# Four more pairs of up units in seven block products, and three input sums moved to GpSimd

## The chip, the cores and the metric

The kernel runs on one core of one Trainium2 chip. The metric is the time of one execution on the device, in microseconds (us). Before the change it is 2313.94 us, the median of three runs (2313.18 to 2315.19).

## What is computed

Two small language-model blocks, one after the other, on an input of 512 tokens by 1024 features, in float32. The first block has two layers (a hybrid of sliding-window attention and a gated delta rule; a gated linear recurrence), each followed by a layer norm, an MLP and another layer norm. The second has two more layers with their own mixers and feed-forward parts. The change touches only the MLP of the first block, which runs twice (`l` = 0 and 1):

```python
def sqrelu_mlp(x, w1, w2):
    h = jax.nn.relu(x @ w1)          # 512x1024 by 1024x4096
    return (h * h) @ w2              # 512x4096 by 4096x1024

for layer in range(2):
    x = layer_norm(a * x + mixer(x), ln1_g[layer], ln1_b[layer])
    x = layer_norm(a * x + sqrelu_mlp(x, mlp_w1[layer], mlp_w2[layer]), ...)
```

## The kernel before

**Layout.** Features lie on the partitions and tokens in the free dimension. `X` holds 8 tiles of 128 features by 512 tokens. A *unit* is 128 output features: its weights are 8 blocks (K blocks) of 128x128, one slot of 1024 columns. `XHS` and `XLS` are the input split into a high part (`XH`, rounded to fp32r) and the rest (`XL`). Weights are split in the same way into `WH` and `WL`. A product is then three matmuls: high by high, high by rest, rest by high (`three`, lines 331 to 333; `product_pe`, lines 1150 to 1152). An ordinary unit takes 8 x 3 matmuls of 512 columns.

**The weight ring.** `plan_units` lists all units in the order in which TensorE uses them. Unit `u` lies in slot `u % 7`. SyncE loads it (`load_weights`, line 274) once unit `u - 7` is done, ScalarE makes the high part (`split_hi`, line 289) and VectorE the rest (`split_lo`, line 304). `WL` and `RAW`, the loaded weights, share their memory. The splits are issued by hand between the other steps of the two engines, four or five units ahead of TensorE (`split_for`).

**The MLP.** It has four parts (q = 0 to 3), each with 8 up units (`w1`) and 8 down units (`w2`). An up unit's result is evicted by ScalarE (relu, line 1231), squared by VectorE (line 1292), and split into `H`, high on ScalarE (line 1222), rest on VectorE (line 1276). The down units of q take it as input and are added to `X`. Up to now parts 0 and 1 run unit by unit, then come the 8 down units of part 0. Parts 2 and 3 run in *pairs*: two up units by 512 tokens by 1024 inputs are a 2x2 by 2x2 product of blocks, done with seven block products instead of eight (Winograd's form of Strassen). A block product is 4 K blocks x 3 matmuls of 256 columns. Between the products of a pair stand two down units of the part before.

**What a pair needs.** Sums of weights, made by GpSimd (`weight_sums`, four operations of 128x512, lines 259 to 265) once the pair's first and fourth slot are loaded: `S1` to `S4`, which take two slots of the ring (`s12`, `s4`) that aren't loaded. And sums of inputs, made once in a layer: T1 (X late front less X early front), T2 (X late back less T1), T4 (X early back less T2), T3 (X late back less X late front), each 128x1024 (four tiles of 256 tokens), and each split into high part and rest. T3's parts overwrite `XH` and `XL`, so T3 waits for the last ordinary up unit. T1, T2, T4 are made by VectorE at line 1127 in the second part, after units 1 to 3 of it; ScalarE makes their high parts after units 3 to 5, VectorE their rests after 4 to 6. T3 is made at the beginning of the down units of part 0.

**Copies out of PSUM.** In a pair TensorE runs M1, M5, a third product, then U2 on top of M1's bank. It may overwrite or add to it only when ScalarE has copied M1 (`p_copy`, line 1247). M5's copy is line 1251, U2's is line 1256.

**Order.** Every engine's instructions run in the order in which they are written here; they meet through semaphores. The queue order on ScalarE ahead of the first pair is this:

```python
            split_hi(act, PAIR_AT[l, 0] + 5)
            s1, s2, s3, c1, c2 = pair_tiles()
            for p, (q, j) in enumerate(PAIRS):
                ...
                act.wait_ge(p_mm, (l, p, "M1"))
                ...
                act.e.activation(s1, PS[BANK_P][:, EARLY], ACT.Copy).then_inc(*p_copy.at((l, p, "M1")))
```

**Ahead of the MLP.** The layer norm before it is worked in two halves of 256 tokens. Its last steps are ScalarE's write of `X` (line 626, signal `x_norm`) and VectorE's rest of the input tile (line 602, signal `x_lo`), in turn with TensorE's first three up units (`first_three_pe`), which take the input tiles one by one. GpSimd has a part in the norm (line 613) and then waits for the first pair's weights.

Of the kernel before, what the change touches and what calls it, by code (L numbers as in the profile page):

```python
# [9 lines left out]
ACT = mybir.ActivationFunctionType  # L10
# [44 lines left out]


PARTS = (8, 8, 6)
PAIRS = [(q, j) for q in (2, 3) for j in range(4)]
FFN_PARTS = [("up", 0), ("up", 1), ("dn", 0), ("up", 2), ("dn", 1), ("dn", 2)]


def plan_units():

    plan = [("hyb", i, 8) for i in HYB_ORDER] + [("hwo", i, 8) for i in range(8)]

    def mlp(l):
        def part(name, q):
            return [(f"{name}_{l}", q * 8 + m, 8) for m in range(8)]

        out = part("w1", 0) + part("w1", 1) + part("w2", 0)  # L70
        for p, (q, j) in enumerate(PAIRS):
            m = 8 * q + 2 * j
            out += [(f"w1_{l}", m, 8), (f"s12_{l}", p, 8), (f"s4_{l}", p, 4), (f"w1_{l}", m + 1, 8)]
            out += [(f"w2_{l}", m - 8, 8), (f"w2_{l}", m - 7, 8)]
        return out + part("w2", 3)

    def ffn(l):
        out = []
# [72 lines left out]
def build_program(nc, D):  # L151
    with ExitStack() as ctx:
# [247 lines left out]
        def ready_of(stage, n=8):  # L400
            return [(x_lo, (stage, k)) for k in range(n)]
# [708 lines left out]
        T_HI = {"T1": by256(YR[:, 0:2, :]), "T2": by256(YR[:, 4:6, :]), "T4": by256(TMR[:, 0:2, :]), "T3": XH[:, FRONT, LATE]}  # L1110
        T_LO = {"T1": by256(YR[:, 2:4, :]), "T2": by256(YR[:, 6:8, :]), "T4": by256(TMR[:, 6:8, :]), "T3": XL[:, FRONT, LATE]}

        def x_sum_dve(dve, l, key):

            if key == "T1":
                dve.wait_ge(x_norm, (2 * l, 7, 1))
                a, b = X[:, FRONT, LATE], X[:, FRONT, EARLY]
            elif key == "T2":
                dve.wait_ge(t_raw, (l, "T1"))
                a, b = X[:, BACK, LATE], T_RAW["T1"]  # L1120
            elif key == "T4":
                dve.wait_ge(t_raw, (l, "T2"))
                a, b = X[:, BACK, EARLY], T_RAW["T2"]
            else:
                dve.wait_ge(unit_done, UNIT[f"w1_{l}"][15])
                a, b = X[:, BACK, LATE], X[:, FRONT, LATE]
            dve.e.tensor_tensor(T_RAW[key], a, b, ALU.subtract).then_inc(*t_raw.at((l, key)))

        def x_sum_act(act, l, key):
            act.wait_ge(t_raw, (l, key))  # L1130
            act.e.activation(T_HI[key], T_RAW[key], ACT.Copy).then_inc(*t_hi.at((l, key)))

        def x_rest_dve(dve, l, key):
# [3 lines left out]
        def pair_tiles():  # L1137

            return TM[:, 2, EARLY], TM[:, 2, LATE], TM[:, 3, EARLY], TM[:, 4, :], TM[:, 5, :]
# [15 lines left out]
        def mlp_pe(pe, l):  # L1155
# [19 lines left out]
                return mm  # L1175

            first_three_pe(pe, w1, stage, norm_behind(pe, 2 * l))
            for q in range(2):
                for m in range(8):
                    if q or m >= 3:  # L1180
                        unit(pe, w1[8 * q + m], m % 4, XHS, XLS, ready_of(stage))
                    pe.until[m % 4] = [(h_sq, (l, q, m))]
            for m in range(8):
                down(0, m)
            for b in (BANK_P, BANK_Q, BANK_R):
                claim(pe, b)
            for p, (q, j) in enumerate(PAIRS):
# [27 lines left out]
        def mlp_act(act, l):  # L1215
            w1, w2 = UNIT[f"w1_{l}"], UNIT[f"w2_{l}"]

            def high(q, m, h):
                act.wait_ge(h_sq, (l, q, m))
                if q > 1:  # L1220
                    act.wait_ge(unit_done, w2[8 * (q - 2) + 7])
                act.e.activation(H[:, 16 * (q % 2) + m, :], h, ACT.Copy).then_inc(*h_hi.at((l, q, m)))  # L1222

            for q in range(2):
                for m in range(8):
                    p = 8 * q + m - 2
                    split_for(split_hi, act, w1, 8 * q + m, 3)
                    act.wait_ge(unit_done, w1[8 * q + m])
                    if p >= 0:
                        act.wait_ge(h_sq, (l, p // 8, p % 8))  # L1230
                    act.e.activation(TM[:, 2 + m % 2, :], PS[m % 4][:, :], ACT.Relu).then_inc(*h_relu.at((l, q, m)))
                    high(q, m, TM[:, 4 + m % 2, :])
                    if q and m in (3, 4, 5):
                        x_sum_act(act, l, ("T1", "T2", "T4")[m - 3])
            for m in range(8):
                split_for(split_hi, act, w2, m)
                if m == 0:
                    x_sum_act(act, l, "T3")
            split_hi(act, PAIR_AT[l, 0] + 5)
            s1, s2, s3, c1, c2 = pair_tiles()  # L1240
            for p, (q, j) in enumerate(PAIRS):
                a0 = PAIR_AT[l, p]
                last = p == len(PAIRS) - 1
                act.wait_ge(p_mm, (l, p, "M1"))
                if p:
                    act.wait_ge(p_sum, (l, p - 1, "C11"))
                act.e.activation(s1, PS[BANK_P][:, EARLY], ACT.Copy).then_inc(*p_copy.at((l, p, "M1")))
                act.wait_ge(p_mm, (l, p, "M5"))
                if p:
                    act.wait_ge(p_sum, (l, p - 1, "C22"))  # L1250
                act.e.activation(s3, PS[BANK_R][:, EARLY], ACT.Copy).then_inc(*p_copy.at((l, p, "M5")))
                split_hi(act, a0 + 6)
                act.wait_ge(unit_done, a0 + 1)
                if p:
                    act.wait_ge(p_sum, (l, p - 1, "C12"))
                act.e.activation(s2, PS[BANK_P][:, EARLY], ACT.Copy).then_inc(*p_copy.at((l, p, "U2")))
                high(q, 2 * j, c1)
                split_hi(act, a0 + (9 if last else 10))
                act.wait_ge(unit_done, a0 + 3)
                act.wait_ge(h_lo, (l, q, 2 * j - 1) if j else (l, q - 1, 7))  # L1260
                act.e.activation(c2[:, EARLY], PS[BANK_P][:, EARLY], ACT.Copy).then_inc(*p_copy.at((l, p, "C21")))
                high(q, 2 * j + 1, c2)
                if not last:
                    split_hi(act, a0 + 11)
            for m in range(8):
                split_last(split_hi, act, w2[24:], m, 0)
                v = None if m < 4 else 0
                stat_act(act, 2 * l + 1, m, v, X[:, m, :], mixed(("mlp", l, 3))(m, v))

        def mlp_dve(dve, l, take):  # L1270
# [13 lines left out]
                    dve.wait_ge(x_mix, (("mlp", l, q - 1), m))  # L1284
                    dve.e.tensor_tensor(X[:, m, :], X[:, m, :], PS[m % 4][:, :], ALU.add).then_inc(*x_mix.at((("mlp", l, q), m)))

            for q in range(2):
                for m in range(8):
                    split_for(split_lo, dve, w1, 8 * q + m, 3)
                    r, h = TM[:, 2 + m % 2, :], TM[:, 4 + m % 2, :]  # L1290
                    dve.wait_ge(h_relu, (l, q, m))
                    dve.e.scalar_tensor_tensor(h, PS[m % 4][:, :], 0.0, r, ALU.max, ALU.mult).then_inc(*h_sq.at((l, q, m)))
                    low(q, m, h)
                    if q and 1 <= m < 4:
                        x_sum_dve(dve, l, ("T1", "T2", "T4")[m - 1])
                    if q and 4 <= m < 7:
                        x_rest_dve(dve, l, ("T1", "T2", "T4")[m - 4])
            x_sum_dve(dve, l, "T3")
            dve.wait_ge(t_raw, (l, "T3"))
            for m in range(8):  # L1300
                split_for(split_lo, dve, w2, m)
                add(0, m)
                if m == 1:
                    x_rest_dve(dve, l, "T3")
            split_lo(dve, PAIR_AT[l, 0] + 5)
            s1, s2, s3, c1, c2 = pair_tiles()

            def square(q, m, c, ready):
# [44 lines left out]
            return take  # L1353

        def mlp_pool(pool, l):
            for p in range(len(PAIRS)):
                weight_sums(pool, l, p)
            for m, v in [(m, None) for m in range(4)] + LAST_FOUR[:3]:
                stat_pool(pool, 2 * l + 1, m, v, X[:, m, :], mixed(("mlp", l, 3))(m, v))
# [2484 lines left out]
```

## Time and profile before

| | |
|---|---|
| median of three runs | 2313.94 us (2313.18 to 2315.19) |
| the profiled execution | 2314.27 us, span on the core 2312.2 us |
| TensorE busy | 2289.0 us, 99%, 13578 matmuls |
| weight loads of TensorE | 1954.3 us, 85% (beside the matmuls) |
| VectorE busy | 1481.2 us, 64% |
| ScalarE busy | 1110.8 us, 48% |
| GpSimd busy | 340.1 us, 15% |
| HBM read | 201.93 MB, 88 GB/s over the span |
| chain that ended last | TensorE 88%, VectorE 6%, issue 3%, ScalarE 2%, GpSimd 1% |

How to read it: matmuls are pipelined, and the duration of one (0.39 us for 512 columns) is longer than the distance to the next. The distance from start to start is what counts. The two MLPs lie at about 290 to 640 us and 793 to 1140 us of the span.

### The profile page before, as it was taken

What the parts mean: (1) busy time and instruction counts of PE and PEld (TensorE: products, weight loads), DVE (VectorE), ACT (ScalarE), POOL (GpSimd) and SP (SyncE); (2) the same over time, 40 slices, a digit from 0 to 9 for tenths busy, and PEclk for the clock granted to TensorE, in tenths of its full rate; (3) what the DMA queues carried; (4) which work ended last, traced back from release to release, by engine and by line L of the source; (5) the groups of instructions that cost most, each with busy time, mean ns of one, the idle gap of its engine ahead of it and who ended that gap; (6) DMA issues with size and microseconds to landing.
All of it is one profiled execution on the core that took longest, in us unless ns stands there. A gap on an engine that the chain in (4) does not pass through costs nothing.

```text
span 2312.2 us, 33438 instructions
## 1 busy us (share of the span) xinstructions
PE 2289.0 (99%) x13578; PEld 1954.3 (85%) x13578; DVE 1481.2 (64%) x2282; ACT 1110.8 (48%) x1927; POOL 340.1 (15%) x296
## 2 busy tenths in 40 slices
PE   9989999999999999999999999999999999999999
PEld 7768888899988988998978888888888789888887
DVE  6798765456687764555776777636586547775455
ACT  5656453334367543333555654434254556444342
POOL 0041410221321400221420101100010001110000
PEclk9999999999999999999999999999999999999999
DMA  6220222223222232223221232322321113233222
GB/s 212 80 74 2 70 96 75 99 92 127 100 92 92 77 115 81 93 101 127 85 87 58 72 114 96 100 93 94 97 93 55 56 37 110 92 100 98 95 91 64
DMA packets 60601, 207.56 MB, mean 90 GB/s; under 512 B 7024, under 2 KB 9120, under 8 KB 60320
## 3 DMA queue, kind: packets, MB, share of 16 engines
q1 hardware_dynamic: 59536, 202.40, 26.3%
q0 software_dynamic: 640, 2.76, 0.3%
q8 instruction: 108, 1.77, 0.3%
q14 instruction: 45, 0.37, 0.0%
q10 hardware_dynamic: 272, 0.26, 0.0%
HBM read 201.93 MB, written 2.10 MB: 88 GB/s over the span
## 4 chain that ended last, share of the span: by engine, by line
PE 88%; DVE 6%; issue 3%; ACT 2%; POOL 1%; DMA 0%; SPq 0%; DVEq 0%; POOLq 0%
PE ps L331 25%; PE ps L333 24%; PE ps L332 24%; PE ps L1152 2%; PE ps L1151 2%; PE ps L1150 2%; DVE TM L677 1%; PE ps L3242 1%; PE ps L392 1%; PE ps L3213 1%; PE ps L3226 1%; DVE WL L304 1%; PE ps L394 1%; PE ps L393 1%; DVE XL L781 0%
## 5 line engine op out<-in xcount | busy, mean ns | idle before, releaser
L331 PE MATMUL ps<-XH,WH 128*128 128x512 f32 (+1 forms) x1856 | 691.2, 372 | 8.0 <-DVE WL L954 5.6
L333 PE MATMUL ps<-XH,WL 128*128 128x512 f32 (+1 forms) x1856 | 676.0, 364 | 0.0
L332 PE MATMUL ps<-XL,WH 128*128 128x512 f32 (+1 forms) x1856 | 675.9, 364 | 0.0
L304 DVE TENSOR_TENSOR WL<-RAW,WH 128x1024 fp32r<-128x1024 f32 (+2 forms) x409 | 488.0, 1207 | 282.1 <-ACT WH L289 175.8
L289 ACT ACTIVATE WH<-RAW 128x1024 fp32r<-128x1024 f32 (+2 forms) x409 | 411.8, 1020 | 150.5 <-POOL RAW L261 86.8
L331 PE MATMUL ps<-H,WH 128*128 128x512 f32 (+1 forms) x1200 | 431.2, 359 | 0.0
L332 PE MATMUL ps<-H,WH 128*128 128x512 f32 (+1 forms) x1200 | 429.9, 358 | 0.0
L333 PE MATMUL ps<-H,WL 128*128 128x512 f32 (+1 forms) x1200 | 429.5, 358 | 0.0
L331 PEld LDWEIGHTS ps<-XH,WH 128*128 128x128 f32 x1856 | 350.6, 189 | 74.7 <-issue 8.5
L333 PEld LDWEIGHTS ps<-XH,WL 128*128 128x128 f32 x1856 | 350.6, 189 | 56.1
L332 PEld LDWEIGHTS ps<-XL,WH 128*128 128x128 f32 x1856 | 350.8, 189 | 55.1 <-issue 2.2
L333 PEld LDWEIGHTS ps<-H,WL 128*128 128x128 f32 x1200 | 226.7, 189 | 33.5
L331 PEld LDWEIGHTS ps<-H,WH 128*128 128x128 f32 x1200 | 226.8, 189 | 32.8 <-issue 0.3
L332 PEld LDWEIGHTS ps<-H,WH 128*128 128x128 f32 x1200 | 226.8, 189 | 32.2
L1425 ACT ACTIVATE TM<-TM,VEC 128x512 f32<-128x512 f32 x88 | 71.9, 817 | 196.2 <-DVE TM L1480 196.2
L1454 DVE SCALAR_TENSOR_TENSOR TM<-TM,VEC 128x511 f32<-128x511 f32 (+1 forms) x176 | 131.4, 746 | 3.1
L1523 POOL TENSOR_TENSOR TM<-TM 128x512 f32<-128x512 f32 x38 | 49.0, 1288 | 502.4 <-DVE TM L1454 451.1
L1222 ACT ACTIVATE H<-TM 128x512 fp32r<-128x512 f32 x64 | 40.5, 632 | 98.8 <-DVE TM L1311 70.4
L259 POOL TENSOR_TENSOR RAW<-RAW 128x512 f32<-128x512 f32 x16 | 20.6, 1286 | 439.8 <-DMA RAW<-in_w 439.8
L767 POOL TENSOR_TENSOR X<-X,TM 128x256 f32<-128x256 f32 x20 | 19.4, 971 | 445.0 <-DVE TM L677 372.4
L1465 DVE TENSOR_TENSOR H<-TM,H 128x512 fp32r<-128x512 f32 x44 | 30.5, 692 | 82.8 <-ACT H L1411 82.8
L1480 DVE TENSOR_TENSOR TM<-ps,TM 128x512 f32<-128x512 f32 x88 | 60.4, 687 | 33.5 <-PE ps L333 31.8
(473 smaller groups left out, 3126.1 us busy)
## 6 DMA issues: line engine op xcount, KB each, us to landing
RAW<-in_w SPq DMA_DIRECT2D x128, 512.0 KB, 3.5
RAW<-in_up SPq DMA_DIRECT2D x88, 512.0 KB, 3.5
RAW<-in_dn SPq DMA_DIRECT2D x32, 512.0 KB, 3.4
RAW<-in_hyb SPq DMA_DIRECT2D x20, 512.0 KB, 3.5
RAW<-in_qkv SPq DMA_DIRECT2D x18, 512.0 KB, 3.5
RAW<-in_kvf SPq DMA_DIRECT2D x17, 512.0 KB, 3.5
RAW<-in_rin SPq DMA_DIRECT2D x16, 512.0 KB, 3.4
RAW<-in_dn SPq DMA_DIRECT2D x16, 384.0 KB, 3.0
```

What stands on the lines that cost most here:

```text
L289: act.e.activation(WH[:, s, 0:n], RAW[:, s, 0:n], ACT.Copy).then_inc(*w_hi.at(u))
L304: dve.e.tensor_tensor(WL[:, s, 0:n], RAW[:, s, 0:n], f32(WH[:, s, 0:n]), ALU.subtract).then_inc(*w_lo.at(u))
L331: pe.e.matmul(out, wh, xh, start=first, stop=False)
L332: pe.e.matmul(out, wh, xl, start=False, stop=False)
L333: return pe.e.matmul(out, wl, xh, start=False, stop=last)
L1150: pe.e.matmul(out, wh, xh[k], start=first and k == 0, stop=False, skip_group_check=not first)
L1151: pe.e.matmul(out, wh, xl[k], start=False, stop=False, skip_group_check=not first)
L1152: mm = pe.e.matmul(out, wl, xh[k], start=False, stop=k == 3, skip_group_check=not first)
L1425: act.e.activation(pair[s], TM[:, 6 + s, :], ACT.Identity, bias=vec("fcb", 44 * l + blk), scale=vec("fcw", 132 * l + 3 * blk + 2)).then_in ...
L1454: dve.e.scalar_tensor_tensor(dst[:, 2 - j:T], u[:, 0:T + j - 2], vec("fcw", 132 * l + 3 * blk + j), dst[:, 2 - j:T], ALU.mult, ALU.add).th ...
L1480: dve.e.tensor_tensor(TM[:, 6 + s, :], PS[b][:, :], RS, ALU.mult).then_inc(*f_u.at((l, q, m, s)))
L1523: pool.e.tensor_tensor(g, g, v, ALU.mult).then_inc(*gate_pool.at(("ffn", l, q, m)))
```

## The change

More pairs: `PAIRS` has the parts 1, 2 and 3, so 12 pairs in a layer instead of 8. The order of a layer's units is then the 8 up units of part 0, twelve pairs, in each of which two down units of the part before stand, and the 8 down units of part 3. The 8 down units of part 0 no longer stand in a block of their own: they are in the first four pairs. The plan has 8 more entries in a layer (two slots for sums in each new pair).

T1, T2 and T4 are made by GpSimd, as the first thing in `mlp_pool`, ahead of its weight sums; T1 waits for the last tile of the layer norm. Their high parts are made by ScalarE after units 4 to 6 of part 0, the rests by VectorE after units 5 to 7. T3 stays on VectorE, after the last ordinary up unit, which is now the eighth; its high part stands on ScalarE between the splits and the first pair.

```diff
-PAIRS = [(q, j) for q in (2, 3) for j in range(4)]
+PAIRS = [(q, j) for q in (1, 2, 3) for j in range(4)]
...
-        out = part("w1", 0) + part("w1", 1) + part("w2", 0)
+        out = part("w1", 0)
         for p, (q, j) in enumerate(PAIRS):
...
-                dve.wait_ge(unit_done, UNIT[f"w1_{l}"][15])
+                e.wait_ge(unit_done, UNIT[f"w1_{l}"][7])
                 a, b = X[:, BACK, LATE], X[:, FRONT, LATE]
-            dve.e.tensor_tensor(T_RAW[key], a, b, ALU.subtract).then_inc(*t_raw.at((l, key)))
+            e.e.tensor_tensor(T_RAW[key], a, b, ALU.subtract).then_inc(*raw_sum(key).at((l, key)))
...
             first_three_pe(pe, w1, stage, norm_behind(pe, 2 * l))
-            for q in range(2):
-                for m in range(8):
-                    if q or m >= 3:
-                        unit(pe, w1[8 * q + m], m % 4, XHS, XLS, ready_of(stage))
-                    pe.until[m % 4] = [(h_sq, (l, q, m))]
             for m in range(8):
-                down(0, m)
+                if m >= 3:
+                    unit(pe, w1[m], m % 4, XHS, XLS, ready_of(stage))
+                pe.until[m % 4] = [(h_sq, (l, 0, m))]
             for b in (BANK_P, BANK_Q, BANK_R):
                 claim(pe, b)
...
             for m in range(8):
-                split_for(split_hi, act, w2, m)
-                if m == 0:
-                    x_sum_act(act, l, "T3")
+                split_for(split_hi, act, w1, m, 3)
+                act.wait_ge(unit_done, w1[m])
+                if m > 1:
+                    act.wait_ge(h_sq, (l, 0, m - 2))
+                act.e.activation(TM[:, 2 + m % 2, :], PS[m % 4][:, :], ACT.Relu).then_inc(*h_relu.at((l, 0, m)))
+                high(0, m, TM[:, 4 + m % 2, :])
+                if 4 <= m < 7:
+                    x_sum_act(act, l, ("T1", "T2", "T4")[m - 4])
             split_hi(act, PAIR_AT[l, 0] + 5)
+            x_sum_act(act, l, "T3")
...
             for m in range(8):
-                split_for(split_lo, dve, w2, m)
-                add(0, m)
-                if m == 1:
-                    x_rest_dve(dve, l, "T3")
+                split_for(split_lo, dve, w1, m, 3)
+                r, h = TM[:, 2 + m % 2, :], TM[:, 4 + m % 2, :]
+                dve.wait_ge(h_relu, (l, 0, m))
+                dve.e.scalar_tensor_tensor(h, PS[m % 4][:, :], 0.0, r, ALU.max, ALU.mult).then_inc(*h_sq.at((l, 0, m)))
+                low(0, m, h)
+                if m > 4:
+                    x_rest_dve(dve, l, ("T1", "T2", "T4")[m - 5])
+            split_lo(dve, PAIR_AT[l, 0] + 4)
+            x_sum(dve, l, "T3")
             split_lo(dve, PAIR_AT[l, 0] + 5)
+            x_rest_dve(dve, l, "T3")
...
         def mlp_pool(pool, l):
+            for key in ("T1", "T2", "T4"):
+                x_sum(pool, l, key)
             for p in range(len(PAIRS)):
                 weight_sums(pool, l, p)
```

## Rows read from the trace of the kernel before

**Rows 1.** Page: TensorE's busy time, and its granted clock in 40 slices.

```profile
PE 2289.0 (99%) x13578; PEld 1954.3 (85%) x13578; DVE 1481.2 (64%) x2282; ACT 1110.8 (48%) x1927; POOL 340.1 (15%) x296
PEclk9999999999999999999999999999999999999999
```

**Rows 2.** Waits of TensorE: total us, times, longest; the longest after the start.

```profile
PE ps L2144 <- DVE TM L2267: 1.6, 1, 1.6
```

**Rows 3.** Timeline, TensorE: start, us, line; first `w2` unit, first pair, second pair.

```profile
375.80 0.39 PE L331 MATMUL ps<-H,WH 128*128 128x512 f32 x1
...
419.32 0.28 PE L1150 MATMUL ps<-XH,WH 128*128 128x256 f32 x1
...
440.32 0.28 PE L1150 MATMUL ps<-XH,WH 128*128 128x256 f32 x1
```

**Rows 4.** Timeline of three engines at the end of the norm.

```profile
302.21 0.59 ACT L626 ACTIVATE X<-TM,VEC 128x256 f32<-128x256 f32 x1
302.26 1.22 DVE L304 TENSOR_TENSOR WL<-RAW,WH 128x1024 fp32r<-128x1024 f32 x1
303.40 0.42 DVE L602 TENSOR_TENSOR XL<-X,XH 128x256 fp32r<-128x256 f32 x1
303.87 0.39 PE L331 MATMUL ps<-XH,WH 128*128 128x256 f32 x1
```

**Rows 5.** Timeline, VectorE and GpSimd in the norm's sums, 512 and 256 columns.

```profile
261.24 1.21 DVE L304 TENSOR_TENSOR WL<-RAW,WH 128x1024 fp32r<-128x1024 f32 x1
261.39 2.20 POOL L517 TENSOR_TENSOR TM<-TM,X 128x512 f32<-128x512 f32 x1 [2.36 <-DVE X L1075]
262.37 1.77 DVE L499 TENSOR_TENSOR TM<-TM 128x512 f32<-128x512 f32 x1
...
272.75 1.21 DVE L304 TENSOR_TENSOR WL<-RAW,WH 128x1024 fp32r<-128x1024 f32 x1
272.91 1.65 POOL L517 TENSOR_TENSOR TM<-TM,X 128x256 f32<-128x256 f32 x1 [0.69 <-DVE X L1075]
```

**Rows 6.** Timeline, GpSimd and VectorE in a later norm.

```profile
1310.64 1.25 POOL L767 TENSOR_TENSOR X<-X,TM 128x256 f32<-128x256 f32 x1 [2.01 <-DVE TM L677]
1310.87 0.42 DVE L499 TENSOR_TENSOR TM<-TM 128x256 f32<-128x256 f32 x1
```

**Rows 7.** Timeline: load issued, first weight sum of a layer, VectorE's rest behind them.

```profile
403.19 0.33 SPq L274 DMA_DIRECT2D RAW<-in_w  x1
406.74 1.29 POOL L259 TENSOR_TENSOR RAW<-RAW 128x512 f32<-128x512 f32 x1 [106.45 <-DMA RAW<-in_w]
411.93 1.23 DVE L304 TENSOR_TENSOR WL<-RAW,WH 128x1024 fp32r<-128x1024 f32 x1 [8.04 <-POOL RAW L265]
```

**Rows 8.** Timeline, ScalarE and VectorE: the steps of an up unit, with T2's sum.

```profile
332.48 0.60 ACT L1231 ACTIVATE TM<-ps 128x512 f32<-128x512 f32 x1 [2.50 <-PE ps L333]
...
349.43 0.69 DVE L1292 SCALAR_TENSOR_TENSOR TM<-ps,TM 128x512 f32<-128x512 f32 x1 [1.09 <-ACT TM L1231]
350.15 0.63 ACT L1222 ACTIVATE H<-TM 128x512 fp32r<-128x512 f32 x1 [0.76 <-DVE TM L1292]
350.82 0.69 DVE L1276 TENSOR_TENSOR H<-TM,H 128x512 fp32r<-128x512 f32 x1 [0.70 <-ACT H L1222]
351.43 1.22 DVE L1127 TENSOR_TENSOR Y<-X,Y 128x1024 f32<-128x1024 f32 x1
352.56 1.22 DVE L304 TENSOR_TENSOR WL<-RAW,WH 128x1024 fp32r<-128x1024 f32 x1
```

**Rows 9.** Timeline, ScalarE: T3's high part, and M1's copy of the first pair.

```profile
379.88 1.06 ACT L1131 ACTIVATE XH<-XF 128x1024 fp32r<-128x1024 f32 x1 [0.95 <-DVE XF L1127]
...
420.95 0.38 ACT L1247 ACTIVATE TM<-ps 128x256 f32<-128x256 f32 x1 [6.49 <-PE ps L1152]
```

**Rows 10.** Timeline, TensorE: the first matmul of the kernel and the thirteenth.

```profile
5.59 0.79 PE L331 MATMUL ps<-XH,WH 128*128 128x512 f32 x1 [5.59 <-DVE WL L954]
...
10.72 0.39 PE L331 MATMUL ps<-XH,WH 128*128 128x512 f32 x1
```

More of the change, by code:

```diff
@@ L1111, in build_program, with raw_sum, x_sum @@
         T_LO = {"T1": by256(YR[:, 2:4, :]), "T2": by256(YR[:, 6:8, :]), "T4": by256(TMR[:, 6:8, :]), "T3": XL[:, FRONT, LATE]}
-        def x_sum_dve(dve, l, key):
+        def raw_sum(key):
+            return dve_own if key == "T3" else t_raw
+        def x_sum(e, l, key):
             if key == "T1":
-                dve.wait_ge(x_norm, (2 * l, 7, 1))
+                e.wait_ge(x_norm, (2 * l, 7, 1))
                 a, b = X[:, FRONT, LATE], X[:, FRONT, EARLY]
             elif key == "T2":
-                dve.wait_ge(t_raw, (l, "T1"))
+                e.wait_ge(t_raw, (l, "T1"))
                 a, b = X[:, BACK, LATE], T_RAW["T1"]
             elif key == "T4":
-                dve.wait_ge(t_raw, (l, "T2"))
+                e.wait_ge(t_raw, (l, "T2"))
                 a, b = X[:, BACK, EARLY], T_RAW["T2"]
             else:
-                dve.wait_ge(unit_done, UNIT[f"w1_{l}"][15])
+                e.wait_ge(unit_done, UNIT[f"w1_{l}"][7])
                 a, b = X[:, BACK, LATE], X[:, FRONT, LATE]
-            dve.e.tensor_tensor(T_RAW[key], a, b, ALU.subtract).then_inc(*t_raw.at((l, key)))
+            e.e.tensor_tensor(T_RAW[key], a, b, ALU.subtract).then_inc(*raw_sum(key).at((l, key)))
         def x_sum_act(act, l, key):
-            act.wait_ge(t_raw, (l, key))
+            act.wait_ge(raw_sum(key), (l, key))
             act.e.activation(T_HI[key], T_RAW[key], ACT.Copy).then_inc(*t_hi.at((l, key)))
@@ L1222, in high @@
                 act.e.activation(H[:, 16 * (q % 2) + m, :], h, ACT.Copy).then_inc(*h_hi.at((l, q, m)))
[L1224 to L1234, printed above, removed]
-            for m in range(8):
-                split_for(split_hi, act, w2, m)
-                if m == 0:
-                    x_sum_act(act, l, "T3")
+            for m in range(8):
+                split_for(split_hi, act, w1, m, 3)
[6 more added lines that the diff above has]
+                    x_sum_act(act, l, ("T1", "T2", "T4")[m - 4])
             split_hi(act, PAIR_AT[l, 0] + 5)
+            x_sum_act(act, l, "T3")
             s1, s2, s3, c1, c2 = pair_tiles()
@@ L1285, in add @@
                     dve.e.tensor_tensor(X[:, m, :], X[:, m, :], PS[m % 4][:, :], ALU.add).then_inc(*x_mix.at((("mlp", l, q), m)))
[L1287 to L1299, printed above, removed]
-            for m in range(8):
-                split_for(split_lo, dve, w2, m)
-                add(0, m)
-                if m == 1:
-                    x_rest_dve(dve, l, "T3")
+            for m in range(8):
+                split_for(split_lo, dve, w1, m, 3)
[7 more added lines that the diff above has]
+            x_sum(dve, l, "T3")
             split_lo(dve, PAIR_AT[l, 0] + 5)
+            x_rest_dve(dve, l, "T3")
             s1, s2, s3, c1, c2 = pair_tiles()
```

## The prediction

> **What bounds the kernel now.** I read the page's busy shares first: TensorE works 99% of the span, and its clock row stands at nine tenths or more in all 40 slices, so at the higher level, 2.4 GHz [rows 1]. The list of waits then says how little TensorE waits: the longest wait after the start is 1.6 us [rows 2]. So the time is the sum of TensorE's matmuls, and a change can win only by fewer columns, or lose by making TensorE wait. What the other engines do costs nothing until TensorE stands for it, so after the matmuls are counted I follow VectorE and ScalarE, step by step, to the places where TensorE needs them.
>
> **Term 1, fewer matmuls: a gain of 6.1 us.** The eight `w2` units of the first part run from 375.80 to 419.32, with nothing between: 43.52 / 8 = 5.44 us for a unit of 24 matmuls of 512 columns. The first pair begins at 419.32, the second at 440.32: 21.00 us for seven block products and two `w2` units [rows 3]. The products take 21.00 - 2 x 5.44 = 10.12 us (84 matmuls of 256 columns, 0.120 us each, 1.44 a product). Two ordinary up units take 10.88. A pair saves 0.76 us, and the change makes four more pairs in each of two layers: 8 x 0.76 = 6.1 us. That is less than the eighth of the columns that is saved, since 256 columns cost 0.120 us and 512 cost 0.227. The other work of a pair (weight splits, three sums out of PSUM, four GpSimd sums) already fits: the later pairs repeat what the traced ones do without a wait, and I cost it at nothing. If that cover failed each pair would show over 21.00 us.
>
> **Term 2, T1 on GpSimd beside the last input rest: a loss of 4.3 us.** GpSimd's sums wait for `x_norm` of tile 7, second half. That is ScalarE's write at 302.21, over at 302.80, so T1 is issued at 302.86. At that moment VectorE is in a weight rest (302.26, 1.22 us), and behind it in its queue stands the rest of tile 7 (line 602, at 303.40), which TensorE waits for even now: it ends at 303.82 and the next matmul begins at 303.87 [rows 4]. GpSimd and VectorE can't run two-input SBUF operations together: a 512-column sum on GpSimd that was issued 0.15 us into a 1.21 us weight rest took 2.20 instead of 1.29, and the VectorE addition next in line took 1.77, ending 0.55 after GpSimd's [rows 5]. So GpSimd waits for the operation under way, goes next, and holds the one behind. GpSimd ran 263.59 - 262.45 = 1.14 us alone there; a 256-column one 274.56 - 273.96 = 0.60 [rows 5]; at 0.54 for 256 columns more, the 1024 columns of T1 take 1.14 + 2 x 0.54 = 2.22 us (bounds: 1.14, if length hardly counted, and 2 x 1.29 = 2.6). T1 then runs 303.48 to 305.70, the rest of tile 7, with 0.28 us left to do, ends at 305.98, and the matmul goes at 306.03 instead of 303.87: 2.16 us lost. The second layer has the same order of work. Two layers: 4.3 us. T2 and T4 hold VectorE up for some 4.4 us more, but the weight rest behind them (303.78 now, some 308 then) is due only after another whole unit, at 312, so TensorE doesn't feel them. Taking these sums off VectorE brings nothing: VectorE was idle there.
>
> **The page's rule and the row.** The Trainium skill, "SBUF — State Buffer", section "Who interferes with whom", says that a VectorE instruction with two SBUF inputs and a GpSimd one that reads SBUF exclude each other, and that whichever issues first has the port for its whole length. Here [rows 6] speak a little against it: GpSimd was issued at 1310.64, VectorE's addition at 1310.87, and yet the addition took its plain 0.42 us and GpSimd 1.25. By the rule term 2 is certain; by the row a lead of 0.23 us isn't enough, and the lead here is 0.54. That is the second rival below.
>
> **Term 3, the first pair without its cover: a loss of 9.8 us.** Before, eight `w2` units (43.5 us) lie between the last up unit and the first pair, and in them VectorE and ScalarE make T3, the weight sums and the splits. After, the pair begins as the eighth up unit (m=7) ends. Its fourth product needs `p_copy` M1, and in ScalarE's queue that copy stands behind two weight splits and behind T3's high part, which waits for VectorE. TensorE asks for it three products in, 3 x 1.44 = 4.32 us after the pair begins.
>
> First the least it can be. From the end of unit 7 the chain is: relu 0.63 (it begins 0.2 after), square 0.73, high part 0.66, low part 0.61, rest of T4 1.14, rest of S3 1.14, T3's sum 1.25, its high part 0.97, M1 copy and hand-over 0.43: 7.8 us [rows 8, 9]. (A following instruction begins 0.09 before the end of the one ahead: 351.43 to 352.56 for 1.22.) So 7.8 - 4.3 = 3.5 us is lost even if VectorE had no backlog. That alone is above the 3.04 us that four pairs save in a layer.
>
> But there is a backlog. At m=5 VectorE's split comes to the first pair's weights and waits for GpSimd's four weight sums. They need a load that may start only when unit 4 is done (slot of seven). In the trace this takes 3.55 us from the issue to GpSimd's first sum and 8.74 us to VectorE's start [rows 7]. Unit 7's relu begins at 332.48 [rows 8], so unit 4 is done three units before, at 316.16 now and 318.3 with term 2, so VectorE goes on at 327.05, with unit 5 long done (323.8). From there the two engines work hand to hand [rows 8, 9]: rest of weights 1.14, square 0.73, on ScalarE high part 0.54, T2 high 0.95, S2 high 1.07; rest of S2 1.14, square 0.73, high 0.66, low 0.61, rest of T2 1.14, S4 0.61, square 0.73, high 0.66, low 0.61, rest of T4 1.14, S3 1.14, T3 1.25, T3 high 0.97, M1 0.43: 16.25 us, so M1's copy is there at 343.3. Eight up units lie between unit 7's end and 375.80 [rows 3], which puts that end at 375.80 - 43.52 = 332.3, so the pair begins at 334.4 and wants it at 338.7. TensorE loses 4.6 us. If GpSimd's weight sums and VectorE's low parts get into each other's way as in term 2, both are 0.7 us later: 5.3. I take 4.9, between the two; low bound 3.5. Then M5, U2 and T3's rest come in time one after the other and nothing more is lost in that pair. Two layers: 9.8 us.
>
> **Sum.** -6.1 + 4.3 + 9.8 = +8.0 us on the profiled execution's 2314.27, whose span is 2312.2; it is 0.3 us above the median of 2313.94. Forecast on the median: 2322.
>
> **Rivals.** *The clock falls.* In both layers TensorE stands still for some 4.9 us. The only idle time of that order in the trace is the start, 5.59 us, and after it 512-column matmuls came 0.43 us apart, which is 1.2 GHz: twelve took 5.13 us, to 10.72, instead of 2.72 [rows 10], a cost of 2.4 us. For it: 4.9 is nearer to 5.6 than to the 1.6 us after which the clock stayed up [rows 1, 2]. Against it: the start isn't a fall, and no row shows one. Price 1.2 to 2.4 us for each stop: 2323 to 2327. The Trainium skill ("TensorE: Matmul & The Clock Gate", "What's actually happening") has an idle array fall back to its lower clock until activity lifts it; no run here shows it yet.
>
> *VectorE's rest goes first (the other side: not slower by more than 0.2%).* One place, line 602 at 303.40: if it takes the port ahead of T1, as the addition of [rows 6] did, term 2 is gone and the time is 2313.94 - 6.1 + 9.8 = 2317.6. It decides by whether a lead of 0.54 us suffices; [rows 5] with a lead of 0.98 speak for GpSimd, [rows 6] with 0.23 against.
>
> *No backlog.* The load and the sums could come earlier or the hand-overs be tighter, so that term 3 is 3.5 a layer: 2313.94 - 6.1 + 4.3 + 7.0 = 2319.1.
>
> *Everything is hidden.* Only term 1: 2307.9. M1's copy stands behind T3 in a queue that is executed in order, so I can't see how.
>
> **Chances.** Forecast (2320 to 2323.5) 0.47; clock falls at one or both stops 0.25; VectorE first 0.13; no backlog 0.08; all hidden 0.03; something dearer (over 2328) 0.04. The range leaves out the last two and little else: from 2317, just under the second rival, to 2328, both clock prices on top of the higher term 3. A measurement of this kernel can tell about 0.2%, 4.6 us, from no change; the bounds lie at 2309.3 and 2318.6. Faster 0.04, within 0.2% 0.16 (VectorE first, and part of no backlog), slower 0.80.
>
> **What the profile after will show.** TensorE's list of waits gets two entries that it hasn't now: a matmul of line 331 to 333 on the rest of tile 7 with some 2 us in each layer, and line 1150 on ScalarE's M1 copy with some 4.9 us, twice. The rest of tile 7 itself takes 2.6 us instead of 0.42 beside a GpSimd sum of 2.8. Pairs after the first keep 21.00 us; TensorE has 288 matmuls more. If a stop is followed by half-speed matmuls the granted clock of that stretch falls under 1. I am wrong if the first pair's fourth product follows its third at once, or if the later pairs stretch.

## The result, and the profile after

The changed kernel takes 2329.26 us (median of four runs, 2327.76 to 2330.38), the kernel before 2313.93 (2313.18 to 2315.19). The ratio is 1.0065, with a 95% interval of 1.0048 to 1.0083: slower by some 15 us. The forecast was 2322, slower by 8, with a range up to 2328. The sign was right, the size was half, and the time lies 1.3 us outside the range.

The profiled execution of the changed kernel took 2327.76 us, its span is 2326.0, so 13.8 us more than the span before. From its page, the busy times and TensorE's clock:

```profile
PE 2289.1 (98%) x13864; PEld 1968.1 (85%) x13866; DVE 1507.2 (65%) x2316; ACT 1124.7 (48%) x1959; POOL 399.4 (17%) x334
PEclk9999999999999999999999999999999999999999
```

Beside [rows 1]: TensorE is as busy as before in 14 us more of span. The clock row still shows nine tenths or more in every slice. A slice is 58 us long, and that is too coarse for what happened. GpSimd has 59 us more.

TensorE's list of waits in the changed kernel (total us, times, longest) has two entries which [rows 2]'s list hadn't:

```profile
PE ps L1154 <- ACT TM L1243: 10.0, 2, 5.0
PE ps L331 <- DVE WL L954: 5.6, 1, 5.6
PE ps L331 <- DVE XL L602: 4.2, 2, 2.1
```

Line 1154 is the block product (1150 before), 1243 is M1's copy, 602 is the rest of input tile 7, 954 is the kernel's start. The forecast said 4.9 and 2 us, twice each. The end of the norm, which answers to [rows 4] (timeline: start, us):

```profile
302.72 1.22 DVE L304 TENSOR_TENSOR WL<-RAW,WH 128x1024 fp32r<-128x1024 f32 x1
303.33 2.81 POOL L1131 TENSOR_TENSOR Y<-X 128x1024 f32<-128x1024 f32 x1 [2.59 <-ACT X L626]
303.85 2.58 DVE L602 TENSOR_TENSOR XL<-X,XH 128x256 fp32r<-128x256 f32 x1
306.48 0.39 PE L331 MATMUL ps<-XH,WH 128*128 128x256 f32 x1 [2.10 <-DVE XL L602]
```

GpSimd's T1 was issued in the middle of a weight rest, waited for its end (T1 takes 2.81 us with that wait), and held up the operation behind it: the rest of tile 7 takes 2.58 us instead of 0.42, and TensorE stands for it. The first pair, from the timeline of VectorE, GpSimd and ScalarE (an arrow names what ended the idle time):

```profile
326.84 1.28 POOL L265 TENSOR_TENSOR RAW<-RAW 128x512 f32<-128x512 f32 x1
328.15 1.23 DVE L304 TENSOR_TENSOR WL<-RAW,WH 128x1024 fp32r<-128x1024 f32 x1 [2.43 <-POOL RAW L265]
...
341.71 1.22 DVE L1131 TENSOR_TENSOR XF<-X 128x1024 f32<-128x1024 f32 x1
342.96 1.06 ACT L1135 ACTIVATE XH<-XF 128x1024 fp32r<-128x1024 f32 x1 [2.27 <-DVE XF L1131]
343.93 0.37 ACT L1243 ACTIVATE TM<-ps 128x256 f32<-128x256 f32 x1
```

And from TensorE's:

```profile
339.08 0.28 PE L1156 MATMUL ps<-XH,WL 128*128 128x256 f32 x1
344.34 0.58 PE L1154 MATMUL ps<-YR,WH 128*128 128x256 f32 x1 [4.98 <-ACT TM L1243]
344.73 0.42 PE L1155 MATMUL ps<-YR,WH 128*128 128x256 f32 x1
...
350.06 0.41 PE L1156 MATMUL ps<-XH,WL 128*128 128x256 f32 x1
350.27 0.32 PE L1154 MATMUL ps<-XH,WH 128*128 128x256 f32 x1
350.43 0.28 PE L1155 MATMUL ps<-XL,WH 128*128 128x256 f32 x1
...
363.75 0.28 PE L1154 MATMUL ps<-XH,WH 128*128 128x256 f32 x1
...
384.75 0.28 PE L1154 MATMUL ps<-XH,WH 128*128 128x256 f32 x1
```

VectorE goes on at 328.15, when the last weight sum is there; T3's sum, its high part and M1's copy follow each other; the copy ends at 344.3 and the fourth product begins 5.14 us late. And then come matmuls of 256 columns 0.21 us apart instead of 0.12, up to 350.27. The later pairs keep 21.00 us, 363.75 to 384.75. The table of windows (stretch, busy us of the engines, then TensorE's granted clock) shows what the slow ones are:

```profile
344.00:347.00 3.00, 2.66 (x12) 2.66 (x13) 2.73 (x4) 1.51 (x4) 0.00 (x0) 0.50 0.03 5
347.00:350.00 3.00, 3.00 (x16) 3.00 (x15) 0.23 (x2) 0.38 (x1) 0.00 (x0) 0.50 0.00 0
350.60:352.00 1.40, 1.40 (x11) 1.31 (x11) 0.84 (x3) 0.94 (x2) 0.00 (x0) 1.00 0.64 187
```

The clock was at half, 1.2 GHz, up to 350.3 us. It fell within the stop and not at its end, as the same table shows for its last 0.7 us:

```profile
343.60:344.30 0.70, 0.00 (x0) 0.00 (x0) 0.70 (x2) 0.70 (x3) 0.00 (x0) 0.50 0.00 0
```

The ledger of this execution, read from the starts of stretches on TensorE:

| part | layer 0 | layer 1 |
|---|---|---|
| wait for tile 7's rest (term 2; forecast 2.16) | 2.15 | 2.14 |
| wait for M1's copy (term 3; forecast 4.9) | 5.14 | 5.17 |
| half-speed matmuls after it (first six products 16.49 and 16.02 us instead of 8.63, less the wait) | 2.72 | 2.22 |
| fewer matmuls (term 1; forecast -3.04) | -3.04 | -3.04 |

Together 13.5. The norm's sums (line 523) mark the same places in both traces: from the first of them ahead of an MLP to the first behind it the kernel before takes 346.25 us twice (277.22 to 623.47, 779.92 to 1126.17), the changed kernel 353.22 and 352.73 (277.68 to 630.90, 787.39 to 1140.12), so +7.0 and +6.5, as in the ledger. A drift of 0.46 us is there at the first of these marks, ahead of all that the change touches; that makes 13.9, against 13.8 of the spans.

This drift is a fall of the clock too. At the stop of [rows 2] (line 2144, here 2135) this execution is 0.48 us ahead of the one before (168.41 beside 168.89). Behind that stop the clock is at half, which it wasn't in the kernel before. From the list of waits and the windows of the changed kernel:

```profile
PE ps L2135 <- DVE TM L2258: 1.6, 1, 1.6
169.50:172.80 3.30, 2.97 (x31) 2.39 (x28) 2.86 (x11) 2.21 (x9) 0.00 (x0) 0.50 0.02 5
```

So the same code with the same stop of 1.6 us had a fall behind it in one execution and none in the other, at a price of 0.9 us here.

So three terms were right to within 0.3 us, and 4.9 us in the two MLPs came from the clock. The median of the four runs is 1.5 us above this execution. Where those come from was open, and so was whether the clock's share is the clock's.

### The profile page after: what moved, and what is told of

It reads as the page before. It is cut to its first block, busy times and chain, and to the rows that moved or that the text cites. A ratio compares the mean times of both kernels' runs of the same rounds, so it can differ in the third digit from the quotient of the medians.

```text
span 2326.0 us, 34202 instructions
## 1 busy us (share of the span) xinstructions
PE 2289.1 (98%) x13864; PEld 1968.1 (85%) x13866; DVE 1507.2 (65%) x2316; ACT 1124.7 (48%) x1959; POOL 399.4 (17%) x334
## 4 chain that ended last, share of the span: by engine, by line
PE 82%; DVE 8%; issue 4%; ACT 4%; POOL 1%; DMA 1%; SPq 0%; another core or an unknown queue 0%; DVEq 0%; POOLq 0%
PE ps L331 22%; PE ps L332 21%; PE ps L333 21%; PE ps L1154 3%; PE ps L1156 3%; PE ps L1155 3%; DVE WL L304 1%; DVE TM L677 1%; PE ps L3233 1%; PE ps L392 1%; PE ps L3204 1%; PE ps L3217 1%; PE ps L394 1%; PE ps L393 1%; ACT WH L289 1%
## 5 line engine op out<-in xcount | busy, mean ns | idle before, releaser
L304 DVE TENSOR_TENSOR WL<-RAW,WH 128x1024 fp32r<-128x1024 f32 (+2 forms) x425 | 505.7, 1207 | 322.3 <-ACT WH L289 177.3
L331 PE MATMUL ps<-XH,WH 128*128 128x512 f32 (+1 forms) x1728 | 641.3, 371 | 12.3 <-DVE WL L954 5.6
L333 PE MATMUL ps<-XH,WL 128*128 128x512 f32 (+1 forms) x1728 | 625.9, 362 | 0.0
L332 PE MATMUL ps<-XL,WH 128*128 128x512 f32 (+1 forms) x1728 | 625.5, 362 | 0.0
L331 PEld LDWEIGHTS ps<-XH,WH 128*128 128x128 f32 x1728 | 326.3, 189 | 74.8 <-issue 8.5
L333 PEld LDWEIGHTS ps<-XH,WL 128*128 128x128 f32 x1728 | 326.3, 189 | 50.8
L332 PEld LDWEIGHTS ps<-XL,WH 128*128 128x128 f32 x1728 | 326.6, 189 | 49.9 <-issue 2.2
L1154 PE MATMUL ps<-XH,WH 128*128 128x256 f32 x384 | 109.7, 286 | 0.0
L1155 PE MATMUL ps<-XL,WH 128*128 128x256 f32 x384 | 109.7, 286 | 0.0
L1156 PE MATMUL ps<-XH,WL 128*128 128x256 f32 x384 | 109.7, 286 | 0.0
```

Of the source, the lines that this page charges most:

```text
L304: dve.e.tensor_tensor(WL[:, s, 0:n], RAW[:, s, 0:n], f32(WH[:, s, 0:n]), ALU.subtract).then_inc(*w_lo.at(u))
L331: pe.e.matmul(out, wh, xh, start=first, stop=False)
L332: pe.e.matmul(out, wh, xl, start=False, stop=False)
L333: return pe.e.matmul(out, wl, xh, start=False, stop=last)
L1154: pe.e.matmul(out, wh, xh[k], start=first and k == 0, stop=False, skip_group_check=not first)
L1155: pe.e.matmul(out, wh, xl[k], start=False, stop=False, skip_group_check=not first)
```

## The experiments

Theory A: the three terms of the prediction, and on top of them a fall of the clock after stops of TensorE. Rivals: the slow matmuls have to do with the first pair's operands; the GpSimd sums or the new pairs cost more than the waits. All differences below are of medians on the same chip as the kernel before beside them (2314.7 to 2315.0), and the change itself stands at +15.3 by its own pair; ratios with their intervals are given where they decide. Where two versions ran on different chips, I compare these differences.

**Filling the stop.** Unread matmuls keep TensorE at work while it would wait.

```diff
+                if p == 0:
+                    claim(pe, 7)
+                    for _ in range(24):
+                        pe.e.matmul(PS[7][:, EARLY], XH[:, 0, 0:128], XH[:, 0, EARLY], start=True, stop=True)
                 pe.wait_ge(p_copy, (l, p, "M1"))
```

> The changed kernel with 24 matmuls of 256 columns that nobody reads, into a bank free at that time, put on TensorE right before it waits for M1's copy in the first pair of each layer. They take 24 x 0.12 = 2.9 us of the 5.14 us that TensorE stands idle there. Theory A (the stop makes the granted clock fall, and that costs 2.7 and 2.3 us in the two layers): the M1 copy comes at the same time, the wait that is left is some 2.2 us, matmuls after it stay 0.12 us apart, and the kernel takes some 5 us less than the changed one, about 2324. Rival B (the slow matmuls after the stop come from something else in the first pair, such as the input sums or the weights just written): they stay 0.21 us apart and the time stays at 2329.

Measured: +11.4 us (ratio 1.0049, 1.0036 to 1.0062), 3.9 less than the change's +15.3. Theory A had said 5. The waits left are 2.0 and 1.8 us, and the matmuls behind them run at full speed. But this trace has slow matmuls where the changed kernel's had none: behind the 2.1 us wait for tile 7's rest, in both layers. The windows of the filled run, first the stretch behind the short wait, then the filled stop:

```profile
308.50:311.50 3.00, 3.00 (x8) 2.30 (x7) 2.40 (x2) 0.57 (x2) 2.92 (x2) 0.50 0.89 309
...
346.00:350.00 4.00, 3.58 (x30) 3.58 (x31) 3.32 (x5) 1.97 (x5) 0.00 (x0) 1.00 0.00 0
```

So theory A holds at the long stop (the products and their operands are the same, only the idle time is shorter), and the short one can cost clock too, here 1.7 us in each layer. That I had not expected.

**GpSimd's sums alone.** The kernel before, with T1, T2 and T4 made by GpSimd after the norm, eight pairs as before.

```diff
         def mlp_pool(pool, l):
+            for key in ("T1", "T2", "T4"):
+                x_sum_dve(pool, l, key)
...
-                    if q and 1 <= m < 4:
-                        x_sum_dve(dve, l, ("T1", "T2", "T4")[m - 1])
```

> The kernel before with one part of the change alone: T1, T2 and T4 are made by GpSimd right after the norm, the pairs stay at eight in a layer. Theory A (T1 holds the port that VectorE needs for the rest of input tile 7): TensorE waits some 2.1 us for line 602 in each layer, the clock stays up, +4.3 us, 2318.2. Rival B (the 2.1 us of the changed kernel's trace are swallowed later, as the rest of the kernel has slack): 2314 to 2315. Rival C (GpSimd's three sums cost more than the one wait): over 2319.

Measured: +6.9 us (1.0029, 1.0017 to 1.0040), near rival C. Its trace has the two waits of 2.1 us for tile 7's rest that theory A names and nothing more on the list, but half-speed stretches behind both, as its windows show:

```profile
308.20:310.90 2.70, 2.70 (x7) 2.10 (x7) 2.04 (x2) 0.63 (x2) 2.62 (x2) 0.50 0.95 340
815.00:816.00 1.00, 1.00 (x4) 0.81 (x4) 1.00 (x1) 0.00 (x0) 0.92 (x2) 0.50 0.68 254
```

**The same with that wait filled.** 14 unread matmuls ahead of the ones that wait for tile 7's rest.

```diff
+                        if (v, k, b) == (1, 7, 0) and stage[:3] == "mlp":
+                            claim(pe, 3)
+                            for _ in range(14):
+                                pe.e.matmul(PS[3][:, HALF[0]], XH[:, 0, 0:128], XH[:, 0, HALF[0]], start=True, stop=True)
                         pe.wait_ge(x_lo, (stage, k) if v else (stage, k, 0))
```

> The kernel before with GpSimd's sums alone, and 14 unread matmuls of 256 columns (1.7 us) ahead of the matmuls that wait for the rest of input tile 7. Theory A (the run without them cost 6.9 us, of which 4.3 are the waits and the rest a fall of the clock after a stop of only 2.1 us): the waits end at the same time, no matmul at half speed, + 4.5 us. Rival B (the 2.6 us above the waits are a cost of the three sums themselves): + 6.9 us again.

Measured: +3.8 us (1.0017, 1.0008 to 1.0026), no slow matmul in either MLP. So the sums on GpSimd cost two waits of 2.1 us, and what came on top of them was the clock, some 3 us for both. Rival B is out.

**T1 after tile 7's rest.** The changed kernel with one more wait on GpSimd.

```diff
                 e.wait_ge(x_norm, (2 * l, 7, 1))
+                e.wait_ge(x_lo, (f"mlp{l}", 7))
```

> The changed kernel with one more wait on GpSimd: T1's sum waits also for VectorE's rest of input tile 7. Theory A (port): the rest takes 0.42 us again, the 2.1 us wait of TensorE at the end of the first three units is gone in both layers, nothing else changes, so some 4.3 us less than the changed kernel: about 2325. Rival: T1, T2 and T4 are later by 1 us and hold back the weight sums, and with them the first pair: then the wait for M1's copy grows by as much as was won, 2329.

Measured: +9.2 us (1.0039, 1.0027 to 1.0052), 6.1 less than the change. Its timeline at the end of layer 0's norm: the rest takes its 0.42 us again, T1 follows it.

```profile
304.18 0.42 DVE L602 TENSOR_TENSOR XL<-X,XH 128x256 fp32r<-128x256 f32 x1
304.56 1.23 DVE L304 TENSOR_TENSOR WL<-RAW,WH 128x1024 fp32r<-128x1024 f32 x1
...
304.74 3.33 POOL L1132 TENSOR_TENSOR Y<-X 128x1024 f32<-128x1024 f32 x1 [3.67 <-DVE XL L602]
```

The wait for M1's copy grew from 5.0 to 5.6 us, since TensorE comes 2.15 us earlier and the chain less. 4.3 - 1.1 = 3.2 us are explained by the waits. The other 2.9 would fit falls of the clock that the short stops no longer cause; this run doesn't show it, since the first trace of the changed kernel had none behind its short stops.

**T1 late and the long stop filled.** Both edits, with 28 matmuls.

> Both edits together: T1's sum waits for the rest of input tile 7 (as in the run with that wait), and 28 unread matmuls of 256 columns fill 3.4 us of the wait for M1's copy (5.6 us in that run's trace). Theory A (what is left is terms 1 and 3 of the prediction with their sizes, and the clock's fall was the rest): no matmul at half speed, 2 x 5.6 = 11.2 us of wait less 6.1 us for fewer matmuls, so the kernel before + 5.1 us, and 4 us less than without the filling (+9.2). Rival B (slow matmuls are no matter of the idle time): + 9.2 as without it.

Measured: +5.5 us (1.0026, 1.0016 to 1.0035). There is no slow matmul in either MLP of its trace. This is the cleanest measure of terms 1 and 3 (-6.1 + 2 x 5.6 = +5.1), and 3.8 us less than without the filling: the price of two falls. Rival B is out.

**M1's and M5's copies first.** On ScalarE, ahead of the two weight splits and T3's high part.

```diff
+            act.wait_ge(p_mm, (l, 0, "M1"))
+            act.e.activation(s1, PS[BANK_P][:, EARLY], ACT.Copy).then_inc(*p_copy.at((l, 0, "M1")))
+            act.wait_ge(p_mm, (l, 0, "M5"))
+            act.e.activation(s3, PS[BANK_R][:, EARLY], ACT.Copy).then_inc(*p_copy.at((l, 0, "M5")))
             split_hi(act, PAIR_AT[l, 0] + 5)
             x_sum_act(act, l, "T3")
```

> The changed kernel with ScalarE's copies of M1 and M5 of the first pair put ahead of the two weight splits and of T3's high part. Theory A (the queue order on ScalarE sets the wait, T3's rest is next): the fourth and fifth product run at once, and TensorE waits at the sixth, for T3's rest or for U2's copy, some 3.2 to 3.6 us instead of 5.1. If the clock stays up after that shorter stop, the gain is 2 x (1.7 + 2.5) = 8 us, about 2321; if it still falls, 2 x 1.7 = 3.4 us, about 2326. Rival B (the stop is VectorE's backlog as a whole and only moves): 2329.

Measured: +8.3 us (1.0039, 1.0025 to 1.0053). In its list of waits the wait moved to the sixth product, for T3's rest, and shrank:

```profile
PE ps L1154 <- DVE XL L1139: 6.0, 2, 3.2
```

In the profiled execution no slow matmul follows these two stops of 2.9 and 3.2 us (one of the two short stops has a fall behind it); it took 2320.59 us at a mean clock of 0.999. The others took 2323.19 to 2325.57 at 0.998 to 0.996. So the clock can stay up after a stop of 3 us. That it fell after it in the others is likely from their times, but they have no trace that shows where it fell.

**VectorE not standing at the weight sums.** T1 late, and the rest of the first pair's weights behind T1's rest instead of ahead of unit 5's square. The rests of T1, T2 and T4 also wait for GpSimd's last sum now.

```diff
-                split_for(split_lo, dve, w1, m, 3)
+                if m != 5:
+                    split_for(split_lo, dve, w1, m, 3)
...
             dve.wait_ge(t_hi, (l, key))
+            if key != "T3":
+                dve.wait_ge(t_raw, (l, "T4"))
```

> T1 late, and VectorE's rest of the first pair's weights, at which it waits for GpSimd's four weight sums, one step later: behind unit 5's square, its low part and T1's rest instead of ahead of them. The run with T1 late alone waits 5.6 us for M1's copy. Theory A (some 2 us of that wait is the backlog from standing at the weight sums, the other 3.5 us are the chain from the last up unit's end through T3, as the prediction has it): the wait falls to 3.5 to 4.0 us in each layer, 3.2 to 4 us less than T1 late alone (+9.2), and up to 4 us more if the clock stays up. Rival B (the chain is bound by ScalarE, or by the work itself, not by the stand): the wait stays at 5 us or more, +9.

Measured: +4.3 us (1.0019, 1.0010 to 1.0028), 4.9 less than T1 late alone. Its list of waits:

```profile
PE ps L1157 <- ACT TM L1246: 7.6, 2, 3.8
```

The wait fell by 1.7 us a layer (5.55 to 3.82): that was the stand at the weight sums, and what is left is near the 3.5 us that the prediction named as the least. Behind both stops of this trace are slow stretches (1.6 us lost each). From start to start the product comes 4.0 us late, so -6.1 + 8.0 + 3.2 makes +5.1, beside +5.0 of the spans.

**A down unit before the sixth product.** T1 late, M1 and M5 first, and the first pair's first down unit ahead of the product with T3.

```diff
+                if p == 0:
+                    down(q - 1, 2 * j)
                 pe.wait_ge(p_copy, (l, p, "U2"))
                 times(other, 0, False, BANK_P, "T3", p).then_inc(*p_mm.at((l, p, "U3")))
-                down(q - 1, 2 * j)
+                if p:
+                    down(q - 1, 2 * j)
```

> T1 late, the copies of M1 and M5 ahead of T3's high part on ScalarE, and in the first pair of a layer the down unit before the sixth product instead of behind it, so that 5.4 us of matmuls cover T3's rest. Theory A: T3 is covered; what is late next is the weight rest of that down unit (0.5 to 2 us) and the sum C22 right behind the sixth product (0.7 us), and the clock stays up: the kernel before - 6.1 + 2 x (1.2 to 2.7), so -3.7 to -0.7 us. Rival B (the whole of VectorE's backlog comes back at the down unit, some 3 us or more, with a fall of the clock): + 1 us or more.

Measured: +1.4 us (1.0006, 0.9997 to 1.0015), no difference from the kernel before that can be told, and 2 us above theory A's upper end. T3 is covered. The weight rest of the down unit comes last now, 1.9 us in each layer; its timeline in layer 0:

```profile
341.15 1.22 DVE L304 TENSOR_TENSOR WL<-RAW,WH 128x1024 fp32r<-128x1024 f32 x1
...
342.47 0.47 PE L331 MATMUL ps<-H,WH 128*128 128x512 f32 x1 [1.91 <-issue]
```

I had read it as 0.5 to 2; it is the upper end. The two products with the wait for C22 take 3.65 us instead of 2.88, 0.8 lost, as expected. Theory A left out a third place: the fourth product waits for M1's copy again, since ScalarE is in the middle of the last up unit's high part, and comes 0.5 us late in each layer:

```profile
337.43 0.39 PE L1155 MATMUL ps<-YR,WH 128*128 128x256 f32 x1 [0.31 <-ACT TM L1240]
```

With these three places (0.5, 2.1 and 0.8 us) a layer loses 3.4 us and wins 3.04, and between the marks of line 523 the MLPs take 0.4 us more each. This execution's span is 2313.3, 1.1 above that of before; the last 0.4 us of it are there at 277 us, ahead of the first MLP. The median lies another 1.0 us above this execution.

**Two down units as cover.** Part 1 has three pairs instead of four; its first two up units stay ordinary, and the first two down units of part 0 stand between them and the first pair. T1 is late.

```diff
-PAIRS = [(q, j) for q in (1, 2, 3) for j in range(4)]
+PAIRS = [(1, 1), (1, 2), (1, 3)] + [(q, j) for q in (2, 3) for j in range(4)]
...
-        out = part("w1", 0)
+        out = part("w1", 0) + part("w1", 1)[:2] + part("w2", 0)[:2]
```

> The changed kernel with three pairs in part 1 instead of four: its first two up units stay ordinary, and two down units of part 0 stand between them and the first pair (10.9 us of matmuls as cover). T1 waits for the rest of input tile 7. Theory A (the loss is the missing cover, two down units are enough for a chain of 7.8 us): no wait of TensorE over 0.5 us at the first pair, the clock stays up, 2 x 3 x 0.76 = 4.6 us less than the kernel before. Rival B (the backlog behind the weight sums is longer than the cover): a wait of 1 to 4 us per layer is left and the time is that of before or more.

Measured: 2310.24 us beside 2314.69, -4.45 us (0.9982, 0.9973 to 0.9990). That is term 1 with nothing against it: 6 x 0.76 = 4.6. Between the marks of line 523 its two MLPs take 2.32 and 2.29 us less than before, 4.61 together. In its trace T3's rest ends at 353.05, the first pair begins at 354.79 right on the pitch of the matmuls, and the second 21.00 us later (timeline):

```profile
351.84 1.21 DVE L1142 TENSOR_TENSOR XL<-XF,XH 128x1024 fp32r<-128x1024 f32 x1
...
354.79 0.28 PE L1157 MATMUL ps<-XH,WH 128*128 128x256 f32 x1
...
375.79 0.28 PE L1157 MATMUL ps<-XH,WH 128*128 128x256 f32 x1
```

This version beats both kernels.

**The changed kernel once more.**

> The changed kernel itself once more, beside the run above on one chip. Theory A: + 15 us on the kernel before, of which 8 are the three terms of the prediction; its trace shows 2 to 4 stretches of half-speed matmuls, always after one of the four stops (2.1 us twice, 5.1 us twice) and nowhere else in the two MLPs, and which of the 2.1 us stops are followed by one differs from execution to execution. Rival B: the place and the number of the slow stretches don't follow the stops.

Measured: +15.7 us (1.0064, 1.0051 to 1.0077), five executions from 2327.56 to 2330.88 at mean clocks of 0.997 to 0.995, the faster the higher. The windows of its trace show three slow stretches: none behind the first short stop (the stretch at 307.5), one behind the second, one behind each long stop:

```profile
307.50:311.00 3.50, 3.23 (x18) 2.87 (x19) 3.50 (x3) 0.60 (x1) 3.42 (x2) 1.00 0.43 118
818.50:821.50 3.00, 3.00 (x8) 2.32 (x7) 2.50 (x2) 0.46 (x1) 2.92 (x2) 0.50 0.93 287
346.20:350.90 4.70, 4.70 (x24) 4.70 (x23) 1.93 (x3) 0.99 (x2) 0.00 (x0) 0.50 0.01 3
857.00:859.30 2.30, 2.30 (x13) 2.30 (x12) 1.73 (x3) 0.50 (x2) 0.00 (x0) 0.50 0.02 7
```

So which stops are followed by half clock, and for how long, differs between the two traced executions of this kernel. It explains little of their difference in time, though. Between the marks of line 523 the two MLPs take 13.6 us more than before here and 13.4 in the first trace; of the 1.5 us by which this span is longer, 1.3 are there at 277 us, ahead of the first MLP. Where the rest of the spread lies is open.

## Why the prediction was wrong, step by step

**Term 1 was right.** Pairs of 21.00 us after the first, and -4.45 us measured for six more pairs against 4.6 worked out. That GpSimd, VectorE and ScalarE fit a pair of part 1 as they did the others was right too.

**Term 2 was right in place and size.** 2.16 us said, 2.15 and 2.14 in the ledger; GpSimd's 2.8 and the rest's 2.6 came as written. The rival in which the rest goes first fell: GpSimd led by 0.52 us (303.33 to 303.85) and had its way in both layers of the six traces in which T1 wasn't late. But I had read [rows 6] as if the length of the lead decided, and it doesn't. First two rows of the changed kernel: T2 led by only 0.13 us and held up the weight rest. Then two of the kernel before: the same two operations as in [rows 6], with the same lead, in the same norm, and there GpSimd had its way:

```profile
306.22 2.46 POOL L1131 TENSOR_TENSOR Y<-X,Y 128x1024 f32<-128x1024 f32 x1
306.35 3.41 DVE L304 TENSOR_TENSOR WL<-RAW,WH 128x1024 fp32r<-128x1024 f32 x1
...
1307.71 0.92 POOL L767 TENSOR_TENSOR X<-X,TM 128x256 f32<-128x256 f32 x1 [78.92 <-DVE TM L677]
1307.95 0.96 DVE L499 TENSOR_TENSOR TM<-TM 128x256 f32<-128x256 f32 x1
```

What the Trainium skill says of issue order ("SBUF — State Buffer", section "Who interferes with whom") agrees with these rows and not with [rows 6]; why VectorE went first there stays open. The late-T1 run shows that no more than an order of events was lost.

**Term 3 was right in place, within 0.3 us in size.** The copy of M1 behind T3 was the one that TensorE waited for. VectorE's stand at the weight sums, the backlog, was 1.7 us of it and I had worked out 1.1 to 1.8. The contention of the sums with VectorE's low parts, which I had left at nought to 0.7, came (the low part at 323.95 took 1.78 us, one of the sums 1.74): VectorE went on at 328.15 and not at 327.05, which is 0.6 us late beside the drift.

**The step that failed is the clock.** I named the fall of the clock as a rival with a chance of 0.25, for the two long stops only, at 1.2 to 2.4 us each. It came after both long stops in both traces of the changed kernel, at 1.5 to 2.7 us, and in every one of its nine timed executions the mean clock lay at 0.995 to 0.997. The sum of forecast and clock is 8.0 + 4.9 = 12.9 for the profiled execution, against 13.8 in the spans; the other 0.9 are 0.5 us more of term 3 and the drift ahead of the MLPs. Two errors of weighing made it a rival instead of a term. I held the missing example of a fall against it, though [rows 10] showed both the length and the price, and 4.9 us was far nearer to 5.6 than to 1.6. And I priced only the stops of 5 us: term 2's stop of 2.1 us was above the 1.6 of [rows 2] too, and it cost 1.6 to 1.7 us of clock in both layers of two traces, in one layer of two others, and in none of the first. Nor was 1.6 us a safe length: the changed kernel's own trace has a fall behind that very stop. With four stops priced at up to 2.7 and 1.7 us, which only the runs gave, the upper end would have been 2331, and the likeliest time 2327 to 2329.

**The other rivals.** "No backlog" was a matter of 1.7 us and needed another order of VectorE's work. "Everything is hidden" asks for a cover, and two down units give it.

What stays open: how the clock decides after a stop of 1.6 to 3 us; the traces give examples of both. So does the spread of the executions ahead of the first MLP, up to 1.75 us against the kernel before in these traces.

## What to carry to other kernels

When work that covered a chain on other engines is moved away, walk that chain instruction by instruction to the first matmul behind it: here the least it could cost (3.5 us a layer) already stood above the gain (3.04), and leaving one pair ordinary to keep 10.9 us of cover, together with T1's later start, turned a loss of 15 us into a gain of 4. Price each new stop of TensorE twice, as idle time and as matmuls at half clock behind it; a stop of 2 us can already cost that. And an elementwise operation given to GpSimd isn't free because GpSimd is idle: look at what VectorE has to do for TensorE in the same 2 us.

## What the runs showed of the hardware

Lengths of stops are the idle time of TensorE in the profile; what a fall cost is what the matmuls behind the stop took beyond their distance at full clock.

- After stops of 4.6 to 5.6 us the granted clock was 0.50 in each case traced (six), and 1.5 to 2.7 us were lost; it had fallen before the stop ended. After 3.8 us it fell in both cases (1.6 us lost each), after 2.9 and 3.2 us in neither.
- After stops of 2.1 us (2.4 from start to start of matmuls) it fell in six of ten cases, for 1.6 to 1.7 us lost. In five of the six the fall came only after TensorE was back at work: in the filled run it resumed at 307.03, its matmuls kept full speed up to 308.2, and 512-column matmuls came 0.43 us apart instead of 0.23 from 308.56 to 311.55. In the sixth (GpSimd's sums alone, layer 1) the clock was at 0.50 from 812.8 on, and TensorE resumed at 812.84.
- Stops shortened by unread matmuls to 1.8 to 2.2 us had none behind them in four cases, nor had the two stops of 1.9 us in the down-first run. So the length of a stop alone doesn't tell.
- Outside the MLPs, behind the stop of 1.6 us of [rows 2], it fell in two of the nine traces that have this stop. In the three others, a stretch at 0.50 between 165 and 172 us began earlier, with no idle time over 1.1 us ahead of it since 155 us.
- A 1024-column sum on GpSimd with two inputs takes 2.43 to 3.33 us beside VectorE's work, a 512-column one 1.03 to 2.50; a two-input VectorE operation of 1024 columns that meets them takes up to 3.42 us instead of 1.23.
